# Layer 0 of a conditioned decoder begins with the pool-input projection on rows without their shift

## The reference: what is computed

```python
for l in range(DEPTH):
    mod = cond @ w_ada[l] + b_ada[l]
    sh1, sc1, g1, sh2, sc2, g2 = jnp.split(mod, 6, axis=-1)
    h = modulate(rmsnorm(x, norm1_g[l]), sh1, sc1)      # h * (1 + sc1) + sh1
    x = x + g1[:, None, :] * mixer(h, ...)
    ...
def mixer(h, ...):
    q, k, v, g, u, a_ret, a_pool = jnp.split(h @ w_in, IN_SPLITS, axis=-1)
    y = retention_chunkwise(rotary(q), rotary(k), v)    # four heads
    ...
    y_pool = multiscale_pool(u, ...) @ w_pool_o
def multiscale_pool(u, ...):
    mix = (window_sum / count - u)                      # per channel, over time
```

## Time and profile before

| | us |
|---|---|
| median of 3 runs | 1477.89 (1476.17 to 1478.99) |
| the profiled execution: its time | 1480.72 |
| its span in the trace | 1479.0 |
| TensorE busy in the span | 1442.8 (98%) |
| VectorE busy | 1131.6 (77%) |
| ScalarE busy | 766.5 (52%) |
| TensorE clock granted, mean | 0.997 of full speed |

### The profile page before, as it was taken

How to read it: one execution, slowest core, us unless ns; L and a number is a source line. 1 busy time by engine, 2 the same in 40 slices (tenths; PEclk the granted TensorE clock), 3 DMA queues, 4 the chain that set the end, 5 groups by cost and what they waited for, 6 DMA issues and landing times.

```text
span 1479.0 us, 18826 instructions
## 1 busy us (share of the span) xinstructions
PE 1442.8 (98%) x6819; PEld 1154.0 (78%) x6819; DVE 1131.6 (77%) x1537; ACT 766.5 (52%) x1102; POOL 151.9 (10%) x139
## 2 busy tenths in 40 slices
PE   7999999999999999999989999999999999999997
PEld 2788877778887878888768887878888778888884
DVE  5774686555669999999978557854355799999998
ACT  4333433222347877777633434331234487777774
POOL 0000001000012212111100000100000122112010
PEclk9999999999999999999999999999999999999999
DMA  9856456455557999999956633632243879999995
GB/s 361 300 185 195 164 198 210 144 173 171 186 221 285 395 372 393 378 379 378 357 195 211 196 118 129 208 121 100 85 175 139 316 264 387 380 382 393 370 370 224
DMA packets 107413, 377.49 MB, mean 255 GB/s; under 512 B 16521, under 2 KB 16713, under 8 KB 106548
## 3 DMA queue, kind: packets, MB, share of 16 engines
q1 hardware_dynamic: 90864, 331.39, 61.6%
q0 software_dynamic: 15200, 40.62, 7.6%
q10 hardware_dynamic: 1252, 4.22, 0.8%
HBM read 361.32 MB, written 34.64 MB: 268 GB/s over the span
## 4 chain that ended last, share of the span: by engine, by line
PE 79%; DVE 13%; DMA 3%; ACT 2%; issue 2%; DVEq 1%; ACTq 0%; SPq 0%; POOLq 0%; POOL 0%
PE ps L1801 24%; PE ps L1803 23%; PE ps L1802 23%; DVE w_lo L1539 4%; DVE w_lo_more L1539 2%; PE ps L1886 2%; DMA gate_row<-mod_rows 1%; PE ps L2064 1%; PE ps L2113 1%; PE ps L1955 1%; DVE xgT_lo L1525 1%; DVE y_out L1562 1%; ACT w_hi L842 1%; DMA raw<-w 1%; PE ps L1959 1%
## 5 line engine op out<-in xcount | busy, mean ns | idle before, releaser
L1019 DVE TENSOR_TENSOR w_lo<-raw,w_hi 128x1024 fp32r<-128x1024 f32 x132 | 161.4, 1224 | 212.7 <-ACT w_hi L653 211.5
L653 ACT ACTIVATE w_hi<-raw 128x1024 fp32r<-128x1024 f32 x132 | 139.1, 1058 | 333.3 <-PE ps L1803 332.6
L1539 DVE TENSOR_TENSOR w_lo<-raw,w_hi 128x1024 fp32r<-128x1024 f32 x184 | 217.5, 1223 | 4.8 <-DMA gate_row<-mod_rows 3.9
L1801 PE MATMUL ps<-w_hi,hT_lo 128*128 128x512 f32 x512 | 206.2, 403 | 3.8 <-DVE hT_lo L1122 3.1
L1539 DVE TENSOR_TENSOR w_lo_more<-raw,w_hi_more 128x1024 fp32r<-128x1024 f32 x176 | 208.2, 1223 | 1.3 <-ACT w_hi_more L842 0.4
L1803 PE MATMUL ps<-w_hi,hT_hi 128*128 128x512 f32 x512 | 200.0, 391 | 0.0
L1802 PE MATMUL ps<-w_lo,hT_hi 128*128 128x512 f32 x512 | 199.5, 390 | 0.0
L842 ACT ACTIVATE w_hi<-raw 128x1024 fp32r<-128x1024 f32 x184 | 187.6, 1057 | 11.2 <-DMA raw<-w 6.6
L842 ACT ACTIVATE w_hi_more<-raw 128x1024 fp32r<-128x1024 f32 x176 | 178.4, 1057 | 7.9 <-DMA raw<-w 5.8
L1801 PE MATMUL ps<-hT_hi,w_lo 128*128 128x512 f32 x320 | 130.5, 408 | 0.0
L1803 PE MATMUL ps<-hT_hi,w_hi 128*128 128x512 f32 x320 | 125.0, 391 | 0.0
(11 more groups left out here) (291 smaller groups left out, 2633.7 us busy)
## 6 DMA issues: line engine op xcount, KB each, us to landing
raw<-w SPq DMA_DIRECT2D x590, 512.0 KB, 6.2
h_rows<-h POOLq DMA_DIRECT2D x8, 1024.0 KB, 4.9
ahead<-w SPq DMA_DIRECT2D x4, 2048.0 KB, 11.9
x_state<-x POOLq DMA_DIRECT2D x2, 2048.0 KB, 9.9
y_rows<-x_in ACTq DMA_DIRECT2D x4, 1024.0 KB, 12.2
x<-x_state POOLq DMA_DIRECT2D x4, 1024.0 KB, 7.3
pair_early<-y_rows SPq DMA_DIRECT2D x4, 1024.0 KB, 6.2
x<-x_in SPq DMA_DIRECT2D x4, 512.0 KB, 13.7
```

Source lines behind the costliest of these rows:

```text
L653: act.activation(w_hi[:, q % W_SLOTS], stream_piece(l, q, r), ACT.Copy).then_inc(w_hi_ready, 1)
L1019: v.tensor_tensor(w_lo[:, q % W_SLOTS], stream_piece(l, q, r), w_hi[:, q % W_SLOTS], ALU.subtract).then_inc(raw_used, 1)
L1539: v.tensor_tensor(ring_lo(e * EXP + n), expert_piece(e, n), ring_hi(e * EXP + n), ALU.subtract).then_inc(raw_used, 1)
L1801: pe.matmul(dst, a_lo, b_hi, start=start, stop=False)
```

## The change

Five parts, all but the last in layer 0 alone.

1. Layer 0 gets its own order of groups (`ORDER`): u, q, k, v0, v1, then as before. The sequence of transfers, slots and ada pieces stays; `stored_piece` only says which stored piece a place in the stream reads. Retention stands behind the fifth group (`HEADS_AFTER`), which is v1 in layer 0 and u in layer 1.
2. The opening is new. SyncE loads all of x first, then column 2 (first half of the scale) in halves of 256 columns, then column 3, and columns 0 and 1 (the shift) last. x is scaled by 1/std in place, turned without scale and shift, and the scale enters as a factor for each partition when ScalarE and VectorE read the turned rows (`first_hi`, `first_low`). The scale comes into that form by turning `first_part` (`first_fold`) and summing 4 x 32 columns (`first_scale`). Bias and gain are loaded as 32 rows (`first_rows`), turned at the very start, and kept in `first_turned`.
3. The group u runs on these rows. ScalarE also keeps the scaled rows in `scaled`; when the shift is there, `shifted_high` and `shifted_low` write `hT_hi` and `hT_lo` again with the shift added, for group q and all behind it. The shift's two columns are now made by VectorE (`column_products`) and turned by TensorE (`column_turned`).
4. `x_state` is neither stored nor waited for in layer 0; x is reloaded from the input.
5. In both layers retention waits for the banks of the group before it one at a time, each where it is first written.

```diff
+ORDER = [["u", "q", "k", "v0", "v1"] + NAMES[5:]] + [NAMES] * (DEPTH - 1)
+HEADS_AFTER = 4
-FIRST_COLUMNS = (2, 0, 3, 1)
-FIRST_W = 2
+FIRST_W = 4
...
+            for t in range(NT):
+                x_load(t)
+            for j in range(ADA_PIECES):
+                column_half_load(2, j, 0, left_landed[j])
             first_w_load(0)
+            for j in range(ADA_PIECES):
+                column_half_load(2, j, 1, landed[j])
             first_w_load(1)
+            for j in range(ADA_PIECES):
+                first_load(ADA_PIECES * 3 + j, ADA_PIECES + j)
+            first_w_load(2)
+            first_w_load(3)
+            sp.wait_ge(first_used, 2)
+            for j in range(ADA_PIECES):
+                first_load(j, j)
+            first_q_load(0)
+            first_q_load(1)
+            for j in range(ADA_PIECES):
+                sp.wait_ge(column_used, j + 1)
+                first_load(ADA_PIECES + j, j)
+            first_q_load(2)
+            first_q_load(3)
+            sp.wait_ge(column_used, 2 * ADA_PIECES)
...
+            def first_scale(n, a, c0, c1):
+                v.wait_ge(first_sum, n)
+                parts = ps[:, 7, P * c0:P * c1].rearrange("p (k q r) -> p k q r", q=4, r=32)
+                v.tensor_reduce(first_cols[:, a, c0:c1], parts[:, :, :, 0], AX, ALU.add)
...
+            def first_low(kb):
+                v.wait_ge(unit_hi, SPLIT0["h1"] + kb + 1)
+                v.scalar_tensor_tensor(hT_lo[:, kb], ps[:, 4 + (UNIT0["h1"] + kb) % 2],
+                                       first_cols[:, 2 + kb // 4, kb % 4:kb % 4 + 1], hT_hi[:, kb],
+                                       ALU.mult, ALU.subtract).then_inc(first_lo, 1)
+            def shifted_low(kb):
+                v.wait_ge(shifted_hi, kb + 1)
+                v.scalar_tensor_tensor(hT_lo[:, kb], scaled[:, kb], first_cols[:, kb // 4, kb % 4:kb % 4 + 1], hT_hi[:, kb],
+                                       ALU.add, ALU.subtract).then_inc(shifted_lo, 1)
...
+                        if l == 0 and name == "q" and t == 0:
+                            pe.wait_ge(shifted_lo, 2 * j + 2)
+                        if l == 0 and (name, j, t) == ("q", 1, 1):
+                            column_turned(0, 2)
...
-                pe.wait_ge(acc_free, acc_value(l, NAMES.index("u"), NT - 1))
+                pe.wait_ge(acc_free, acc_value(l, HEADS_AFTER, 0))
                 kv(0)
+                pe.wait_ge(acc_free, acc_value(l, HEADS_AFTER, 1))
                 y_tiles(0, 0, 1)
```

More of the change, by code:

```diff
@@ new lines, in first_shift, with column_products @@
+            def first_shift(n, a):
+                v.wait_ge(first_sum, n)
+                v.tensor_reduce(first_cols[:, a], ps[:, 7].rearrange("p (k r) -> p k r", k=4), AX, ALU.add)
+                v.drain()
+                v.tensor_tensor(first_cols[:, a], first_cols[:, a], first_turned[:, a, 0], ALU.add
+                                ).then_inc(first_cols_ready, 1)
+            def column_products(j, slot, turn, acc):
+                v.wait_ge(landed[slot], 16 * turn)
+                for i in range(2):
+                    piece = raw[:, slot, 512 * i:512 * i + 512]
+                    c = cond[:, 2 * j + i:2 * j + i + 1]
+                    if j == 0 and i == 0:
+                        one = v.tensor_scalar(ada_acc[:, acc], piece, c, None, ALU.mult)
+                    else:
+                        one = v.scalar_tensor_tensor(ada_acc[:, acc], piece, c, ada_acc[:, acc], ALU.mult, ALU.add)
+                    if i == 1:
+                        one.then_inc(column_used, 1)
+                    last = v.drain()
+                if j == ADA_PIECES - 1:
+                    last.then_inc(column_summed, 1)
@@ new lines, in _ @@
+                    lo(0, 4, RAW_OF_W[4])
+                    first_shift(4, 0)
+                    lo(0, 5, RAW_OF_W[5])
+                    shifted_low(0)
+                    shifted_low(1)
+                    column_products(0, 0, 3, 0)
+                    shifted_low(2)
+                    shifted_low(3)
+                    for j in range(1, ADA_PIECES):
+                        column_products(j, j, 3, 0)
+                    lo(0, 6, RAW_OF_W[6])
+                    first_shift(5, 1)
@@ L1689, in _ @@
+                    shifted_low(4)
+                    shifted_low(5)
+                    lo(0, 7, RAW_OF_W[7])
+                    shifted_low(6)
+                    shifted_low(7)
                     v.drain()
@@ L1887, in transposes, with first_transposes, first_products, column_turned @@
                 one.then_inc(unit_ready, 1)
[L1889 to L1898 removed]
+            def first_transposes(kb):
+                bank = unit(0, "h1", kb)
+                if kb >= 2:
+                    pe.wait_ge(first_lo, kb - 1)
+                for t in range(NT):
+                    if kb == 0:
+                        pe.wait_ge(h_ready, t + 1)
+                    one = pe.transpose(bank[:, t * P:(t + 1) * P], x[:, t, kb * P:(kb + 1) * P], ident)
+                one.then_inc(unit_ready, 1)
+            def first_products(j, tiles):
+                pe.wait_ge(first_lo, 2 * j + 2)
+                for t in tiles:
+                    product(0, 0, j, t)
+            def column_turned(acc, n):
+                pe.wait_ge(column_summed, n)
+                pe.wait_ge(first_cols_ready, n + 2)
+                for i in range(4):
+                    one = pe.transpose(ps[:, 7, i * P:(i + 1) * P], ada_acc[:, acc, i * P:(i + 1) * P], ident)
+                one.then_inc(first_sum, 1)
             def norm_transposes(l, t):
@@ new lines, in first_second_scale @@
+            def first_second_scale():
+                for c in range(8):
+                    j, i = divmod(c, 2)
+                    if i == 0:
+                        pe.wait_ge(landed[ADA_PIECES + j], 16)
+                    if c == 0:
+                        pe.wait_ge(first_part_ready, 2)
+                    quadrant = slice(32 * (c % 4), 32 * (c % 4) + 32)
+                    mm = pe.matmul(ps[quadrant, 6], cond_wide[:, c], raw[:, ADA_PIECES + j, 512 * i:512 * i + 512],
+                                   start=c < 4, stop=c >= 4)
+                mm.then_inc(first_used, 1)
@@ new lines, in first_fold @@
+            def first_fold(part):
+                pe.wait_ge(first_part_ready, part + 1)
+                if part == 2:
+                    pe.wait_ge(first_cols_ready, 2)
+                for i in ((0, 1), (2, 3), (0, 1, 2, 3))[part]:
+                    one = pe.transpose(ps[:, 7, i * P:(i + 1) * P], first_part[:, i * P:(i + 1) * P], ident)
+                one.then_inc(first_sum, 1)
+            pe.wait_ge(consts_landed, 16)
+            pe.wait_ge(first_rows_landed, 16)
+            pe.transpose(ps[:, 7, 128:160], first_rows[:], ident[0:32, 0:32]).then_inc(first_turned_ready, 1)
```

414 lines of the change are left out of this document (188 added, 226 removed).

## The result

| | us |
|---|---|
| changed kernel, median of 5 runs | 1468.83 (1468.61 to 1470.03) |
| kernel before, median of 5 runs beside it | 1476.17 (1475.82 to 1478.99) |
| ratio after / before | 0.995, 95% interval 0.9939 to 0.996 |
| the profiled execution: its time, its span | 1468.83, 1467.2 |

The change makes the kernel faster by 7.3 us. Of the 2.9 us between 1471.7 and 1468.83, 1.7 are the reference, which was 1477.89 by three executions and is 1476.17 by five, and 1.1 are the gain, 7.3 instead of 6.2. In a later comparison, with both kernels timed again, the medians were 1470.44 and 1477.22, ratio 0.9959 (0.9945 to 0.9973); that one lies inside.

The account below looks back on a forecast made before the run. TensorE, four fifths of the last-ending chain, was taken to bound the kernel. Gain of 6.7 us in the opening, less 0.35 and 0.15, made -6.2; 1477.9 - 6.2 = 1471.7 us, range 1469.3 to 1475.2.

Parts of the forecast that it names:

- first group: Layer 0's opening: 28.5 us of TensorE work from the first product at 19.4, so the group ends at 47.9.
- second group: Layer 0's second group: one more turn on TensorE costs 0.35 us, with nothing else lost if VectorE keeps up.
- The start: Layer 0's opening: the first product starts at 19.4 us, against 22.29 before.
- Deviations, halves and scalings: Ahead of the first product: deviations end at 13.7, half-wide columns at 13.3, scalings at 14.8, within 1.5 us of each other.
- Parts 4 and 5: Dropping the x_state store in layer 0 and waiting tile by tile at retention: each claimed to give nothing.
- The weight stream: SyncE's queue stops until near 54.7; the third group's piece still has six us to spare, so it costs nothing.
- the slower rival: Second group: shift-column pieces at twice the price on VectorE erase the gain, at three times 1484 us; chance 0.03.
- the third y tile waits for ScalarE's states, so I count 0.15 of loss: Layer 0's retention: two copies of v1's last tile make ScalarE's next work about 0.15 us later.
- The first group's last ends where the second group starts, at 54.61: Kernel before, layer 0: the first group's products were taken to run from 22.29 to 54.61, 32.3 us.
- 0.3 to spare: Second group's shift: VectorE needs 10.7 us until the second column is summed, TensorE reaches its turn after 11.0.
- The clock: Rival in the opening: half clock over the first products loses 3.2 us, gain 3.0, time 1474.9; chance 0.08.
- the opening of before had gaps of the same kind and shows 1.00 throughout: Argument against half clock over the first products: the old opening's similar gaps left the granted clock at 1.00.

Follow-up runs that it names:

- after_shift_pad: Changed kernel with two unused 128x512 VectorE passes added between the pieces of the second shift column; median 1471.90 us, ratio 0.9968 to the kernel before.
- before_fill_later: Kernel before with ScalarE's four issues of the y_rows loads moved behind head_deviations; 1475.85 against 1477.15 us, ratio 0.9991.
- after_better_later: Changed kernel with ten more filler matmuls, deviations not awaiting constants, table behind the third scaling, and y_rows issues behind head_deviations; median 1468.53 us.
- after_better_4: Changed kernel with four more filler matmuls, deviations not awaiting constants, table behind the fourth scaling, y_rows issues behind head_deviations; 1467.93 us, ratio 0.9928 to the kernel before.
- after_all_banks: Changed kernel with part 5 undone, so retention waits once for all four banks; 1470.71 us, ratio 0.9959 to the kernel before.
- the next kernel: Kernel before with part 4 alone: x neither stored to x_state nor waited for in layer 0; ratio 1.0007 to the kernel before.
- after_no_busy: Changed kernel without the opening's eight filler matmuls (two after the columns, six after the turns of x); 1471.10 us, ratio 0.9958 to the kernel before.
- after_better: Changed kernel with ten more filler matmuls, ScalarE's deviations not waiting for the constants, and the table made behind the third scaling; median 1469.02 us.

## Why the prediction came out too small

Means of the four unchanged profiles of before and the two of after, in us, beside the forecast (a minus is a gain):

| stage | forecast | first pair of profiles | means |
|---|---|---|---|
| first product | -2.9 | -2.56 | 22.47 to 19.68: -2.8 |
| first group | -3.8 | -4.39 | -4.4 |
| second group | +0.35 | +0.64 | +0.65 |
| groups three to five | 0 | -0.10 | -0.1 |
| scores to `state` | +0.15 | -1.23 | 4.68 to 4.21: -0.5 |
| routing of layer 0 | 0 | +0.35 | +0.35 |
| until layer 1's selection | -6.2 | -7.71 | 1168.81 to 1162.11: -6.7 |

The rows of the first pair add up to -7.3; the other 0.4 us fall between 450 and 1160 us and were not looked for.

**Right, in part by luck.** The start: 19.4 forecast, 19.35 to 19.42 at the full clock, by the copy at 15.3 and 4.1 us behind it (forecast: 14.8 and 4.6). Two errors of 0.5 us cancel there, and that is luck. Deviations, halves and scalings met within 1.5 us as said, but both chains to the copy were late: ScalarE's because the constants came 1.1 us later than 7.46 (behind which four times 1.51 are 13.5, not the 13.7 that was written), VectorE's because the small load came 1.1 us later than 10 and the table took 0.7 instead of 0.4; that a tile's deviation took 1.40 instead of about 1.5 us and a scaling 0.90 instead of 1.1 gave part of it back. Parts 4 and 5 at nothing, each shown by a kernel of its own within the runs' 0.15%. The weight stream at nothing: groups three to five differ by 0.1. The place in the second group at which it is tight, and that the slower rival's price per microsecond is full: shown by the pad.

**The step that failed: "the third y tile waits for ScalarE's states, so I count 0.15 of loss".** I priced ScalarE's next work by the copies ahead of it and did not look at the row between: its four issues of `y_rows`, 4.65 us long in the trace of before. They, and not the copies, set when ScalarE's states are written. Matmuls that read `state` wait until ScalarE is through them; behind `head_deviations` they cost nothing (3.94 in before_fill_later, after_better_later and after_better_4). The term came out as a gain of 0.5 in the means and of 1.2 in the first pair. That the new order makes the issues shorter is not shown: over all profiles with the issues in their old place the distances are 3.94 to 5.37 in the old order (six profiles) and 4.00 to 4.81 in the new (nine), and they overlap. So the wait that I had wrong is shown, and whether its gain belongs to the new order is open.

**Terms that were mis-sized.** The first group was forecast at -3.8 and gave -4.4, which is as much of the miss as the states are. "The first group's last ends where the second group starts, at 54.61" was a misreading: the first group ends at 55.99 (the 97th matmul of the products in the trace), one product later. The new end, forecast 47.9, was 49.04: 0.3 from the start, 0.8 from the group. There the columns, folds and turns between the products took 6.24 us, less than the forecast's 6.4, but the products 23.07 instead of 22.1: ten of their 96 matmuls, most of them the first behind an interruption, are followed 0.31 to 0.47 us later instead of 0.23. The errors of the two ends, 1.4 and 1.1 us, nearly cancel, to a gain of 6.95 instead of 6.7 at the boundary. The second group cost 0.3 more than its turn. And "0.3 to spare" was 0.0.

**What is scatter.** The reference itself: 1477.89 was the median of three runs, 1476.17 of five, and 1477.00 to 1478.49 in the four later comparisons. So the first comparison met the lowest reference of the five, 1.7 us under the one I used. The sum of the range did not cover that: gains of 4.8 to 7.5 give 1470.4 to 1473.1 and not 1470.2 to 1473.3, and the lower bound, 1469.3, takes off 0.9 and not the 1.4 that is named for scatter. Part of the scatter has a place: stretches at the lower clock behind the selection of layer 1 (after_all_banks shows 0.59 from 1164 to 1168 us) in four of the 18 profiles, and around 740 us, where layer 0 passes into layer 1, in five. They fall in one execution and not in the next. Three of the four are among the seven profiles of the old order; whether the order has a part in that is not shown. Ratios of 0.995 and 0.9959 with intervals that overlap need no cause of their own. What remains open is what makes the four issues last 2.8 us once and 4.7 the next time.

**The clock.** The rival was put at 0.08 for a loss over the first products. The fillers in the opening prevent that, as the kernel without them shows; what they don't prevent is slow folds and turns, 0.3 us in two of the four profiles of this opening. The reason I gave against it, "the opening of before had gaps of the same kind and shows 1.00 throughout", did not bear the weight: the same opening showed 0.50 in the next kernel. The Trainium skill (TensorE: Matmul & The Clock Gate, Part 1) states that half rate is the default until activity releases it; the 0.43 between starts in after_no_busy agrees, and the 1.00 that its window prints does not.

## What to carry to other kernels

Where several chains meet at a start, write down for each what its first instruction waits for: here deviations waited for 470 KB of constants to get one number, and scalings for a table that was wanted 5 us later, together 0.6 to 0.9 us of the start. Because the two ended together, mending one of them alone could not have given that. A row of DMA issues on a compute engine's queue is work on that engine: price it at the longest duration seen, and look for it before saying what the engine's next work costs. A single profile is one draw: check the landmark on which a sum rests in a second one, and count to the boundary of a stage instead of reading it off.

## What the runs showed of the hardware

- The granted clock printed for a window can be 1.00 where matmuls start 0.43 us apart (after_no_busy, 20 to 22 us), the spacing that goes with 0.50 in the earlier trace rows. So read the spacing of equal matmuls beside the window.
- The old opening starts the first product 0.8 us apart (22.3 to 22.7 against 23.2 and 23.3) according to whether matmuls are slow behind a wait of TensorE for a landing, and with four matmuls in that wait the median was 2.4 us lower (ratio 0.9982).
- Loads in runs of 1 KB landed 0.75 us per 256 KB, whole pieces 1.28 per 512 KB: 17% more for each byte. The Trainium skill (DMA: Bandwidth & Descriptors, Specifications) gives 512 B as the least transfer for full rate, and the row does not agree with it; loads of 256 KB in longer runs were not tried, so whether the runs or the size of the loads is the cause is open.
- An issue of four loads from ScalarE's queue took 2.77 to 4.65 us at the same place.
- VectorE stood still for 0.43 us in layer 0's routing, with nothing to wait for:

```profile
426.01 0.18 DVE L1414 TENSOR_TENSOR beats<-lg 128x16 f32<-128x16 f32 x1
426.62 0.42 DVE L1443 TENSOR_REDUCE ranks<-beats 128x64 f32<-128x256 f32 x1 [0.43 <-issue]
```

  It is in every profile whose VectorE program has the changed kernel's length, and in none of before or where instructions were added ahead of it (after_shift_pad, after_better and its followers): the 0.35 us of the table's routing row. The instructions at this spot are the same in all of them; that the place of the code is the cause is a guess that no run tested by itself.
